# Scan inverse in two 64x64 diagonal parts, in a hybrid encoder layer

## Chip, cores, metric

The kernel runs on one core of one Trainium2 chip. The metric is the device time of one execution in microseconds (us); smaller is better.

## The reference, cut to what matters

One layer: an input projection of x (256 tokens x 1024), three mixers in parallel (gMLP, bidirectional RWKV-7, bidirectional mLSTM), an output projection and a norm, then a mixture of 32 experts and a second norm. The change is in RWKV-7, whose state for each of six heads of 64 channels follows

```python
def _wkv7_step(state, inp):
    r, w, k, v, a, b = inp
    sa = jnp.einsum('phvk,phk->phv', state, a)
    state = state * w[:, :, None, :] + sa[..., None] * b[:, :, None, :] + v[..., None] * k[:, :, None, :]
    return state, jnp.einsum('phvk,phk->phv', state, r)
```

once forward and once backward over the 256 tokens.

## The kernel before

The scan is done in chunks of 128 tokens. Within a chunk the products of keys and queries give a strictly triangular 128x128 matrix M, and the values U that enter the state are the product of the inverse Y of (identity - M) with W, what the earlier state and the values give. A pass handles one pair of heads (`pt` = 0, 1, 2), and in it four matrices (two heads x two chunks, index `j = 2h + c`) for each of two directions `d`.

Y is built by doubling, over `LEVELS = (1, 2, 4, 8, 16, 32, 64)`. Level n joins neighbouring diagonal blocks of m = LEVELS[n] rows and columns to blocks of 2m. `neighbours` (level 0) brings Y with its nearest entries into a bank of PSUM (four matrices x 128 columns = 512 columns) by transposes. At each further level, for each direction: ScalarE has copied Y out of the bank (`turned_in`), with its "late" columns in the first 256 columns of `ym` and its "early" ones in the other 256. TensorE turns the early half (`turn_early`, two transposes) and multiplies the early columns of M by the late ones of Y (`cross`, two matmuls of 128 columns). ScalarE copies the turned half to `tT`; VectorE masks the product to the diagonal blocks (`masked`, 256 columns, into `gm`). `update` adds tT by gm to the late columns of the bank (two matmuls). POOL lays out M's early columns for each level ahead (`early_columns`, four buffers `m_early`). In the profile, a 32-bit matmul appears as two records (two passes), a transpose as one.

Directions are interleaved in an order written out by hand: level n of direction 0, level n of direction 1, then side work of the mLSTM and gMLP mixers (`m_rows`, `scores`, `bonus_sums`, `gate_cols`, `scans_turned` on TensorE, `args` and `factors` on ScalarE, divisions, norms and weights on VectorE), then the updates of both directions. After the levels, two steps over the chunks follow: W (`L1205`, `L1207`), U (`L1219`: Y by W, two matmuls of 64 columns for each direction), the state (`L1226`, `L1227`), and at the end the scan's output (`L1236`, `L1240`, `L1242`). `L1052` is the mLSTM's `weigh`, between W and U of step 0 and also ahead of the neighbours of the later passes; `L1111` are the key products.

Lines of the levels: `L1120` neighbours, `L1128` cross, `L1135` turn_early, `L1143` update, `L799`/`L801` turned_in, `L817` the copy to tT, `L1748` the mask, `L1467` POOL's copies, `L1763` VectorE's masking of the products into `mp`, after which `s_prev` is raised. `L1030` is m_rows, `L1038` scores, `L786` args.

Later: the output projection (`L1257`), the router, and the experts (`L1373` and `L1405` for the two expert matrices, `L1347` combining, `L1357` bias rows), whose weights of 12 MB an expert SyncE loads in pieces into slots as these come free.

Of the kernel before, what the change touches and what calls it, by code (L numbers as in the profile page):

```python
# [14 lines left out]
P = 128  # L15
# [4 lines left out]
HD = 64  # L20
# [14 lines left out]
NL = len(LEVELS)  # L35
# [9 lines left out]
C_BONE = NKEEP  # L45
C_MASK2 = C_BONE + P
C_GM = C_MASK2 + 2 * 3 * P
C_X1 = C_GM + NL * P
C_HSEL = C_X1 + 2 * P
C_SELM = C_HSEL + 2  # L50
# [3 lines left out]
def constants():  # L54

    c = np.zeros((P, NCONST), np.float32)
    i = np.arange(P)
    row, col = i[:, None], i[None, :]
    c[:, C_ID:C_ID + P] = row == col
    c[:, C_TRI0:C_TRI0 + P] = row < col  # L60
    c[:, C_BONE:C_BONE + P] = row // HD == col // HD
    for d in range(2):
        before = (row < col) if d == 0 else (row > col)
        o = C_MASK2 + 3 * P * d
        c[:, o:o + P] = before
        c[:, o + P:o + 2 * P] = before | (row == col)
        c[:, o + 2 * P:o + 3 * P] = before.T
        c[:, C_X1 + d * P:C_X1 + d * P + P] = (row // 2 == col // 2) & (row % 2 == 1 - d) & (col % 2 == d)
    for n, m in enumerate(LEVELS):
        c[:, C_GM + n * P:C_GM + n * P + P] = (row // HD == col // HD) & (row % HD // m == col % HD // m)  # L70
    c[:, C_HSEL:C_HSEL + 2] = row // HD == np.arange(2)[None, :]
    for h in range(RH):
        c[h, C_SELM + h * P:C_SELM + (h + 1) * P] = 1.0
    c[:, C_ONES:C_ONES + P] = 1.0
    c[:, C_IOTA:C_IOTA + P] = np.arange(P)[None, :] % SLOTS
    return c
# [30 lines left out]
def encoder_kernel(nc, t, out, dbg=None):  # L107
# [6 lines left out]
    with ctx:  # L114
# [125 lines left out]

        nqT = rview(2, 0, 2, 4, 256)
        mp = rview(2, 2048, 2, 2, 4, P)
        m_early = [view(o_xT + 512 * b, 2, 2, P) for b in range(4)]
        ym = rview(3, 0, 2, 4, P)
        oT = rview(3, 3584, NCH, P)
        tT = rview(3, 1024, 2, 2, P)
        gm = rview(3, 2048, 2, 2, P)
        bktok = rview(3, 3072, 2, 2, P)

# [91 lines left out]
            a = a.rearrange("p j (b two m) -> p two (j b) m", two=2, m=LEVELS[n])  # L341
            return a if d else a[:, ::-1]

        def by_late(a, d, n):
            return a.rearrange("p j s -> p (j s)").rearrange("p (two b m) -> p two b m", two=2, m=LEVELS[n])

        def half_cols(a, n):

            return a.rearrange("p a (b m) -> p (a b) m", m=LEVELS[n])

        def y_late(d):
            return ym[:, d, 0:2].rearrange("p a (b s) -> p (a b) s", b=2)

        def y_early(d):
            return ym[:, d, 2:4]

        def key_bank(pt, d, h):

# [53 lines left out]
        s_nqe = sem("key_products_evacuated")  # L412
        s_yid = sem("identity_laid")
        s_xup = sem("inverse_evacuated")
        s_me = sem("early_columns_of_operand_ready")
        s_tt = sem("early_columns_turned")
        s_tev = sem("early_columns_evacuated")
# [230 lines left out]
        def _(act):  # L648
# [145 lines left out]
            def turned_in(pt, n, d):  # L794

                act.wait_ge(s_xn, 2 * NL * pt + 2 * n + d + 1)
                y = pview(1 + 4 * d, 0, 4, P)
                if n < NL - 1:
                    A(by_late(ym[:, d], d, n + 1), split(y, d, n + 1), ACT.Copy).then_inc(s_xup, 1)  # L799
                else:  # L800
                    A(ym[:, d], y, ACT.Copy).then_inc(s_xup, 1)  # L801

            def identities():

# [5 lines left out]
            for pt in range(NP):  # L810
                for n in range(1, NL):
                    if n == 1:
                        for d in range(2):
                            turned_in(pt, 0, d)
                    for d in range(2):
                        act.wait_ge(s_tt, 12 * pt + 2 * n + d - 1)
                        A(tT[:, d], pview(4 * d + 2, 0, 2, P), ACT.Copy).then_inc(s_tev, 1)  # L817
                        if n == 2:
                            A(bktok[:, d], pview(4 * d + 2, 256, 2, P), ACT.Copy).then_inc(s_bkev, 1)
                    if n == 3:  # L820
                        if pt == 0:
# [106 lines left out]
        def _(pe):  # L928
# [158 lines left out]
            for pt in range(NP):  # L1087
# [28 lines left out]
                def neighbours(d):  # L1116

                    pe.wait_ge(s_prev, 4 * pt + 2 * d + 2)
                    for j in range(4):
                        last = mm(pview(4 * d + 1, 0, 4, P)[:, j], ym[:, d, j], ident, is_transpose=True, start=(j == 0),  # L1120
                                  stop=False, skip_group_check=True)
                    last.then_inc(s_xn, 1)

                def cross(n, d):

                    pe.wait_ge(s_me, 12 * pt + 2 * n + d - 1)
                    for jj in range(2):
                        last = mm(pview(4 * d, 0, 2, P)[:, jj], m_early[(n - 1) % 4][:, d, jj],  # L1128
                                  y_late(d)[:, 2 * jj:2 * jj + 2], start=True, stop=True)
                    last.then_inc(s_a, 1)  # L1130

                def turn_early(n, d):

                    for jj in range(2):
                        last = tr(pview(4 * d + 2, 0, 2, P)[:, jj], y_early(d)[:, jj], ident)  # L1135
                    last.then_inc(s_tt, 1)

                def update(n, d):

                    pe.wait_ge(s_g, 12 * pt + 2 * n + d - 1)  # L1140
                    pe.wait_ge(s_tev, 12 * pt + 2 * n + d - 1)
                    for jj in range(2):
                        last = mm(part(pview(4 * d + 1, 2 * P * jj, 2, P), n, 1 - d), tT[:, d, jj], gm[:, d, jj],  # L1143
                                  start=False, stop=(n == NL - 1), skip_group_check=True)
                    last.then_inc(s_xn, 1)

                key_products(0)
# [7 lines left out]
                for n in range(1, NL):  # L1155
                    for d in range(2):
                        if n == 1 and d == 1:
                            neighbours(1)
                        if n == 1:
                            pe.wait_ge(s_nqe, 4 * pt + (2 if pt else 1) + d)  # L1160
                        if n == 2:
                            tr(pview(4 * d + 2, 0, 4, P)[:, 2], bt[:, d, d], ident)
                            tr(pview(4 * d + 2, 0, 4, P)[:, 3], kt[:, d, d], ident).then_inc(s_bk, 1)
                        if n == 3:
                            pe.wait_ge(s_bkev, 2 * pt + d + 1)
                        pe.wait_ge(s_xup, 2 * NL * pt + 2 * (n - 1) + d + 1)
                        turn_early(n, d)
                        cross(n, d)
                    if n == 1 and pt == NP - 1:
                        pe.wait_ge(s_gv, 1)  # L1170
                        pe.wait_ge(s_nqe, 4 * pt + 4)
# [26 lines left out]
                for step in range(2):  # L1198
# [13 lines left out]
                    for d in range(2):  # L1212
                        c = d if step == 0 else 1 - d
                        pe.wait_ge(s_wev, 4 * pt + 2 * step + d + 1)
                        if step == 0:
                            pe.wait_ge(s_xup, 2 * NL * pt + 2 * (NL - 1) + d + 1)
                        for h in range(2):
                            j = 2 * h + c
                            last = mm(pview(4 * d + 2, 256, 4, HD)[:, j], ym[:, d, j], wbuf[:, d, j], start=True, stop=True)  # L1219
                        last.then_inc(s_u, 1)  # L1220
                    if step == 0:
                        for d in range(2):
# [212 lines left out]
        def _(pool):  # L1435
# [21 lines left out]

            def early_columns(pt, n):

                if n > 4:  # L1460
                    pool.wait_ge(s_a, 12 * pt + 2 * (n - 4))
                elif n == 1 and pt:
                    pool.wait_ge(s_a, 12 * pt)
                for d in range(2):
                    if n == 1:
                        pool.wait_ge(s_prev, 4 * pt + 2 * d + 2)
                    nc.gpsimd.tensor_copy(half_cols(m_early[(n - 1) % 4][:, d], n), part(mp[:, d, 1], n, d)).then_inc(s_me, 1)  # L1467

            for pt in range(NP):
                if pt == NP - 1:  # L1470
# [1 line left out]
                    pool.dma_start(rw, t["router_w"][0].rearrange("(k p) e -> p k e", p=P)).then_inc(s_rw, 16)  # L1472
                    pool.dma_start(rb, row_bc(t["router_b"][0])).then_inc(s_rw, 16)
                    pool.dma_start(lncol, t["ln1_cols"].rearrange("p (a k) -> p a k", a=2)).then_inc(s_rw, 16)
                for n in range(1, NL):
                    early_columns(pt, n)
                mask_factors(2 * pt)
                mask_factors(2 * pt + 1)
# [14 lines left out]
        def _(dve):  # L1493
# [250 lines left out]
            for pt in range(NP):  # L1744
# [11 lines left out]
                for d in range(2):  # L1756
                    near = scan_const(C_X1 + P * d, P).bitcast(i32)
                    dve.wait_ge(s_yid, 2 * pt + d + 1)
                    for h in range(2):
                        dve.wait_ge(s_prod, 4 * pt + 2 * d + h + 1)  # L1760
                        V.copy_predicated(ym[:, d, 2 * h:2 * h + 2], wide(near, 2), pview(4 * d + h, 0, 2, 2, P)[:, :, 1])
                    for h in range(2):
                        V.tensor_tensor(mp[:, d, :, 2 * h:2 * h + 2].rearrange("p a c s -> p c a s"), pview(4 * d + h, 0, 2, 2, P),  # L1763
                                        wide(mask_mp(d).rearrange("p (a s) -> p a s", a=2), 2), ALU.mult).then_inc(s_prev, 1)
                    if d == 0 and pt:
# [296 lines left out]
```

## Time and profile before

| | |
|---|---|
| median of 3 runs | 1202.96 us (1202.22 to 1203.02) |
| profiled execution: time, span | 1202.76 us, 1200.7 us |
| TensorE busy | 1146.5 us (95% of the span) |
| VectorE, ScalarE, POOL busy | 287.5, 216.5, 32.7 us |
| read from HBM | 429.29 MB, 358 GB/s over the span |
| scan passes end at | 151.9, 190.8, 230.7 us |

Times within the profile count from the start of the span; the profiled execution's time is 2.06 us more than its span. The passes' ends are where the chain of waits leaves the last L1242 of each pass. A busy share is an average over stages, so what a stage is worth has to be read in it.

### The profile page before, as it was taken

The page shows a single profiled execution, that of the slowest core. Times are in us where ns is not written, and L with a number is a line of the kernel's source. Part 1 is how long each engine was busy: PE and PEld are TensorE (multiplying, and loading weights), DVE is VectorE, ACT ScalarE, POOL GpSimd, SP SyncE. Part 2 cuts the span into 40 slices and gives each one's busy share as a digit, 9 for nine tenths or more (in the row PEclk, how much of TensorE's full clock was granted, in tenths as well). Part 3 has the DMA queues.
Part 4 walks back from the last instruction along what each step waited for, and adds up shares of the span by engine and source line. Part 5 has one row for each costly group of instructions (what it writes and reads, how often), then busy time and mean ns, then how long its engine had stood idle before and what let it go on. Part 6 is the DMA issues. An engine that isn't in the chain of part 4 may idle for free.

```text
span 1200.7 us, 14572 instructions
## 1 busy us (share of the span) xinstructions
PE 1146.5 (95%) x5836; PEld 503.0 (42%) x5836; DVE 287.5 (24%) x742; ACT 216.5 (18%) x453; POOL 32.7 (3%) x67
## 2 busy tenths in 40 slices
PE   7999999999999999999999999999999999999995
PEld 6875878753333333333333333333333333333332
DVE  1368566662111111111111111111111111111113
ACT  1345554411111111111111111111111111111112
POOL 1000122100000000000000000000000000000001
PEclk9999999999999999999999999999999999999999
DMA  8525202289999999999999999999999999999994
GB/s 334 201 104 203 101 1 77 111 325 364 408 428 430 428 428 428 428 431 428 428 429 428 428 384 425 429 428 428 428 428 428 428 428 428 428 428 428 427 428 172
DMA packets 34025, 430.69 MB, mean 359 GB/s; under 512 B 3808, under 2 KB 3968, under 8 KB 7888
## 3 DMA queue, kind: packets, MB, share of 16 engines
q1 hardware_dynamic: 32736, 427.15, 84.8%
q0 software_dynamic: 544, 2.06, 0.5%
q10 hardware_dynamic: 720, 1.15, 0.3%
q8 instruction: 16, 0.26, 0.1%
q14 instruction: 9, 0.07, 0.0%
HBM read 429.29 MB, written 1.05 MB: 358 GB/s over the span
## 4 chain that ended last, share of the span: by engine, by line
PE 59%; DMA 32%; DVE 5%; ACT 1%; issue 1%; SPq 1%; POOL 0%; POOLq 0%; DVEq 0%
PE bank L1373 19%; DMA pool<-in_exp_w 17%; DMA ring<-in_exp_w 15%; PE bank L1405 14%; PE bank L958 5%; PE bank L968 3%; PE bank L1347 2%; PE bank L1257 2%; PE bank L1357 2%; PE bank L1391 1%; DVE pool L1974 1%; DVE pool L1969 1%; PE bank L1128 1%; PE bank L1143 1%; DVE pool L1971 1%
## 5 line engine op out<-in xcount | busy, mean ns | idle before, releaser
L1405 PE MATMUL bank<-ring,pool 128*64 128x512 f32 x1024 | 228.4, 596 | 9.3 <-DMA ring<-in_exp_w 9.2
L1373 PE MATMUL bank<-pool 128*64 128x512 f32 x1024 | 228.2, 595 | 7.0 <-DMA pool<-in_exp_w 6.7
L1373 PE MATMUL bank<-ring,pool 128*64 128x512 f32 x1024 | 228.0, 595 | 5.9 <-DMA ring<-in_exp_w 5.6
L1405 PEld LDWEIGHTS bank<-ring,pool 128*64 128x64 f32 x1024 | 70.1, 137 | 165.8 <-issue 145.0
L1373 PEld LDWEIGHTS bank<-pool 128*64 128x64 f32 x1024 | 71.2, 137 | 159.3 <-issue 143.5
L1373 PEld LDWEIGHTS bank<-ring,pool 128*64 128x64 f32 x1024 | 71.2, 137 | 158.1 <-issue 143.1
L1955 DVE TENSOR_SCALAR pool<-pool 128x128 f32<-128x128 f32 x64 | 19.3, 346 | 428.6 <-PE bank L1373 428.6
L898 ACT ACTIVATE pool<-pool 128x512 f32<-128x512 f32 x32 | 20.2, 632 | 473.1 <-DVE pool L1967 473.1
L1967 DVE TENSOR_SCALAR pool<-bank 128x512 f32<-128x512 f32 x32 | 22.2, 693 | 317.6 <-PE bank L1373 317.6
L958 PE MATMUL bank<-pool,ring 128*128 128x256 f32 x272 | 61.4, 388 | 7.1 <-DMA ring<-in_w_in_C 7.1
L1347 PE MATMUL bank<-pool 64*128 64x512 f32 x264 | 65.6, 614 | 0.7 <-ACT pool L908 0.7
L908 ACT ACTIVATE pool<-bank 128x512 f32<-128x512 f32 x32 | 19.2, 599 | 258.3 <-PE bank L1405 258.3
L1333 PE MATMUL bank<-pool 128*64 128x512 f32 x264 | 62.3, 592 | 1.0 <-DVE pool L1928 1.0
L958 PEld LDWEIGHTS bank<-pool,ring 128*128 128x128 f32 x272 | 52.8, 195 | 14.9 <-DMA ring<-in_w_in_C 7.1
L1357 PE MATMUL bank<-pool 32*64 32x512 f32 x392 | 44.8, 613 | 0.0
L1347 PEld LDWEIGHTS bank<-pool 64*128 64x128 f32 x264 | 22.7, 185 | 43.1 <-issue 41.5
L968 PE MATMUL bank<-ring,pool 128*128 128x384 f32 (+2 forms) x96 | 35.3, 528 | 0.0
L1333 PEld LDWEIGHTS bank<-pool 128*64 128x64 f32 x264 | 18.9, 137 | 38.2 <-issue 37.1
L900 ACT ACTIVATE pool<-bank 128x512 f32<-128x512 f32 x32 | 19.2, 599 | 66.4 <-PE bank L1333 66.4
L1969 DVE TENSOR_SCALAR pool<-bank 128x512 f32<-128x512 f32 x32 | 22.2, 693 | 32.8 <-PE bank L1373 32.8
L1257 PE MATMUL bank<-ring,pool 128*128 128x512 f32 x64 | 28.5, 596 | 0.8 <-ACT pool L857 0.8
L1391 PE MATMUL bank<-pool 128*128 128x128 f32 x128 | 24.0, 310 | 3.5
(300 smaller groups left out, 858.2 us busy)
## 6 DMA issues: line engine op xcount, KB each, us to landing
ring<-in_exp_w SPq DMA_DIRECT2D x127, 2048.0 KB, 22.2
pool<-in_exp_w SPq DMA_DIRECT2D x64, 2048.0 KB, 27.0
ring<-in_w_out SPq DMA_DIRECT2D x2, 2048.0 KB, 7.6
ring<-in_w_in_A SPq DMA_DIRECT2D x1, 2048.0 KB, 13.5
ring<-in_w_in_B SPq DMA_DIRECT2D x1, 2048.0 KB, 7.8
ring<-in_w_in_D SPq DMA_DIRECT2D x1, 2048.0 KB, 13.3
ring<-in_w_in_H SPq DMA_DIRECT2D x1, 2048.0 KB, 8.0
ring<-in_exp_w SPq DMA_DIRECT2D x2, 1024.0 KB, 22.3
```

The costliest lines, as they stand in the source:

```text
L898: A(sg, hr, ACT.Sigmoid, scale=1.702).then_inc(s_hs, 1)
L958: last = mm(bank[i % 4][:, 0:S], w[:, k], xT[:, k], start=(k == 0), stop=(k == KD - 1))
L968: last = mm(bank[(NT + j) % 4][:, 0:n], xT[:, k, P * c:P * c + P], w[:, k, :], start=(k == 0), stop=(k == KD - 1))
L1257: last = mm(bank[4 + 2 * c + hf][:, :], xT[:, k, P * c:P * c + P], wout[hf][:, OUT_ORDER[k // 2][k % 2]], start=(k == 0), stop=(k == KD - 1))
L1333: last = mm(bank[7][SLOTS * hf:SLOTS * hf + SLOTS, :], sel[:, c], x_tok[:, c, 512 * hf:512 * hf + 512], start=(c == 0), stop=(c == NCH - 1))
L1347: last = mm(bank[2 * c + hf][:, :], gT[hp, P * c:P * c + P], ysb[hp, :], start=False, stop=stop, skip_group_check=True)
L1357: last = mm(bank[4 + g][SLOTS * hf:SLOTS * hf + SLOTS, :], esel[gp], bias[gp, 512 * hf:512 * hf + 512], start=True, stop=False)
L1373: last = mm(bank[4 + g][hp, :], lhs, w[:, k % 2, o:o + 512], start=False, stop=(k == KD - 1))
L1391: last = tr(pview(4, 0, 4, P)[:, j], hr[:, j:j + 509:4], ident)
L1405: last = mm(bank[6][SLOTS * hf:SLOTS * hf + SLOTS, :], hT[:, k % 4, SLOTS * (k // 4):SLOTS * (k // 4) + SLOTS], w2s[k // 4][:, k % 4, 512 ...
L1967: V.tensor_scalar(hr, bank[4][:, :], 7.0, None, ALU.min).then_inc(s_hg, 1)
L1969: V.tensor_scalar(ur, bank[5][:, :], 7.0, -7.0, ALU.min, ALU.max).then_inc(s_hu, 1)
```

## The change

The inverse is no longer kept as 128x128 until the last level. For the levels up to m = 16 (n = 1 to 5) only its two diagonal 64x64 parts are kept, stacked on the partitions: four matrices x 64 columns = 256 columns of the bank for each direction. The neighbours are now real matmuls with a folding matrix `C_FOLD` (128x64). Each level has one transpose (four matrices x 32 early columns = 128 columns), two products, one for each 64-row block (operand `m_early[:, d, b]`), a mask of 256 columns as before, and two updates of 64 stationary columns into the 64 partitions of their block; the copies by ScalarE are 256 and 128 columns wide instead of 512 and 256. The last level (n = 6) fills the block between the two parts: its operand `m_last` is copied by ScalarE from the products, and its result is `y_last`, with the later diagonal part copied beside it. U is computed by two matmuls instead of one for each matrix: the rows that come first from their own 64x64 part, the later rows from `y_last`. There are three buffers of `m_early` instead of four, and POOL makes two copies instead of one for each level and direction, at five levels instead of six.

```diff
-        m_early = [view(o_xT + 512 * b, 2, 2, P) for b in range(4)]
+        m_early = [view(o_xT + 512 * b, 2, 2, P) for b in range(3)]
+        m_last = view(o_xT + 1536, 2, 4 * HD)
...
             def turned_in(pt, n, d):
                 act.wait_ge(s_xn, 2 * NL * pt + 2 * n + d + 1)
-                y = pview(1 + 4 * d, 0, 4, P)
-                if n < NL - 1:
-                    A(by_late(ym[:, d], d, n + 1), split(y, d, n + 1), ACT.Copy).then_inc(s_xup, 1)
+                if n < NL - 2:
+                    A(by_late(y_blocks(d), n + 1), split(y_bank(d), d, n + 1), ACT.Copy).then_inc(s_xup, 1)
+                elif n == NL - 2:
+                    A(y_blocks(d), bank[4 * d + 1][:, 0:4 * HD], ACT.Copy).then_inc(s_xup, 1)
                 else:
-                    A(ym[:, d], y, ACT.Copy).then_inc(s_xup, 1)
+                    first = rows_of(d)
+                    A(y_last(d)[first], pview(4 * d + 1, 4 * HD, 4, HD)[first], ACT.Copy).then_inc(s_xup, 1)
...
                     if n == 1:
                         for d in range(2):
+                            later, first = rows_of(1 - d), rows_of(d)
+                            for h in (1, 0):
+                                act.wait_ge(s_prev, 4 * pt + 2 * d + 2 - h)
+                                A(m_last[later, d].rearrange("p (j s) -> p j s", j=4)[:, 2 * h:2 * h + 2],
+                                  pview(4 * d + h, 0, 2, 2, P)[later, :, 1, first], ACT.Copy).then_inc(s_ml, 1)
                             turned_in(pt, 0, d)
                     for d in range(2):
                         act.wait_ge(s_tt, 12 * pt + 2 * n + d - 1)
-                        A(tT[:, d], pview(4 * d + 2, 0, 2, P), ACT.Copy).then_inc(s_tev, 1)
+                        A(tT[:, d], bank[4 * d + 2][:, 0:P], ACT.Copy).then_inc(s_tev, 1)
...
+                    if n == NL - 1:
+                        for d in range(2):
+                            later = rows_of(1 - d)
+                            A(y_last(d)[later], y_bank(d)[later], ACT.Copy).then_inc(s_yl, 1)
...
                 def neighbours(d):
                     pe.wait_ge(s_prev, 4 * pt + 2 * d + 2)
+                    pe.wait_ge(s_ml, 4 * pt + 2 * d + 1)
                     for j in range(4):
-                        last = mm(pview(4 * d + 1, 0, 4, P)[:, j], ym[:, d, j], ident, is_transpose=True, start=(j == 0),
-                                  stop=False, skip_group_check=True)
+                        last = mm(y_bank(d)[:, j], ym[:, d, j], scan_const(C_FOLD, HD), start=(j == 0), stop=False,
+                                  skip_group_check=True)
...
+                def level(n, d):
+                    pe.wait_ge(s_me, 10 * pt + 2 * n + d - 1)
+                    if n == 1:
+                        pe.wait_ge(s_ml, 4 * pt + 2 * d + 2)
+                    tr(bank[4 * d + 2][:, 0:P], y_early(d), ident).then_inc(s_tt, 1)
+                    for b in range(2):
+                        last = mm(pview(4 * d, 0, 2, P)[:, b], m_early[(n - 1) % 3][:, d, b], y_late(d), start=True, stop=True)
+                    last.then_inc(s_a, 1)
+
+                def last_level(d):
+                    first, later = rows_of(d), rows_of(1 - d)
                     for jj in range(2):
+                        last = tr(bank[4 * d + 2][:, HD * jj:HD * jj + HD], y_blocks(d)[first, P * jj:P * jj + P],
+                                  ident[first, first])
+                    last.then_inc(s_tt, 1)
+                    for jj in range(2):
+                        last = mm(pview(4 * d, 0, 2, P)[:, jj], m_last[later, d, P * jj:P * jj + P],
+                                  y_blocks(d)[later, P * jj:P * jj + P], start=True, stop=True)
                     last.then_inc(s_a, 1)
...
+                    if n < NL - 1:
+                        for b in range(2):
+                            bp = rows_of(b)
+                            last = mm(part(y_bank(d)[bp], n, 1 - d), tT[:, d, bp], gm[:, d, b], start=False, stop=False,
+                                      skip_group_check=True)
+                    else:
+                        for jj in range(2):
+                            o = 4 * HD + P * jj
+                            last = mm(bank[4 * d + 1][rows_of(d), o:o + P], tT[:, d, HD * jj:HD * jj + HD], gm[:, d, jj],
+                                      start=False, stop=True, skip_group_check=True)
...
                         for h in range(2):
                             j = 2 * h + c
-                            last = mm(pview(4 * d + 2, 256, 4, HD)[:, j], ym[:, d, j], wbuf[:, d, j], start=True, stop=True)
+                            u = pview(4 * d + 2, 256, 4, HD)[:, j]
+                            mm(u[first], y_block(d, j)[first], wbuf[first, d, j], start=True, stop=True)
+                            last = mm(u[later], y_last(d)[:, j], wbuf[:, d, j], start=True, stop=True)
...
                 for d in range(2):
                     if n == 1:
                         pool.wait_ge(s_prev, 4 * pt + 2 * d + 2)
-                    nc.gpsimd.tensor_copy(half_cols(m_early[(n - 1) % 4][:, d], n), part(mp[:, d, 1], n, d)).then_inc(s_me, 1)
+                    m = m_early[(n - 1) % 3][:, d]
+                    for b in range(2):
+                        cols = mp[:, d, 1, :, rows_of(b)].rearrange("p j (b two m) -> p two j b m", two=2, m=LEVELS[n])[:, d]
+                        last = nc.gpsimd.tensor_copy(m[:, b].rearrange("p (j b m) -> p j b m", j=4, m=LEVELS[n]), cols)
+                    last.then_inc(s_me, 1)
```

## Rows read from the trace of the kernel before

**Rows 1.** The page's slices of the span: mean busy share of the DMA engines, in tenths.
```profile
DMA  8525202289999999999999999999999999999994
```

**Rows 2.** Windows of the expert stage: busy time and instructions, clock, DMA share, GB/s.
```profile
400.00:800.00 400.00, 389.15 (x1894) 135.05 (x1891) 53.24 (x127) 44.67 (x84) 0.00 (x0) 1.00 1.00 425
```

**Rows 3.** Timeline of SyncE's DMA queue: start, us, engine, line, operation.
```profile
244.18 0.91 SPq L557 DMA_DIRECT2D pool<-in_exp_w  x2
```

**Rows 4.** Chain of waits, middle pass, its start and levels 1 to 3: start, us, what.
```profile
154.78 1.48 PE bank L1052 x12
156.26 0.45 PE bank L1120 x4
156.70 1.06 PE bank L1111 x8
...
160.69 0.42 DVE ring L1748
...
163.59 0.43 DVE ring L1748
...
164.07 1.16 PE bank L1143 x8
165.23 1.06 PE bank L1030 x4
...
167.63 1.35 ACT pool L786 x4
```

**Rows 5.** Timeline of the middle pass, level 5, direction 0, to level 6.
```profile
173.46 0.44 PE L1135 MATMUL bank<-pool,ring 128*128 128x128 f32 x2 [0.24 <-ACT ring L799]
...
174.45 0.42 DVE L1748 TENSOR_TENSOR ring<-bank,pool 128x256 f32<-128x256 f32 x1 [1.18 <-PE bank L1128]
174.59 0.38 ACT L817 ACTIVATE ring<-bank 128x256 f32<-128x256 f32 x1 [0.28 <-PE bank L1135]
...
175.67 1.20 ACT L799 ACTIVATE ring<-bank 128x512 f32<-128x512 f32 x2 [0.36 <-PE bank L1143]
...
176.32 0.44 PE L1135 MATMUL bank<-pool,ring 128*128 128x128 f32 x2
```

**Rows 6.** Chain of waits, middle pass, from W of step 0 to the scan's output.
```profile
180.02 0.84 PE bank L1207 x8
180.86 1.34 PE bank L1052 x12
182.20 0.89 PE bank L1219 x8
...
186.46 1.04 PE bank L1219 x8
...
188.94 0.42 PE bank L1242 x2
189.36 0.37 PE bank L1236 x4
189.73 0.22 PE bank L1240 x4
```

**Rows 7.** Chain of waits in the expert stage.
```profile
305.90 3.43 PE bank L1373 x16
309.33 1.92 PE bank L1347 x8
```

**Rows 8.** Chain of waits, first pass: VectorE ahead of the second direction's neighbours.
```profile
116.60 1.19 DVE ring L1763 x2
```

**Rows 9.** Groups of instructions of the scan, shapes kept apart: xcount, busy us, mean ns, idle before.
```profile
L1467 POOL COPY pool<-ring 128x256 f32<-128x256 f32 x36 | 13.5, 418 | 119.7 <-DVE ring L1763 112.5 <-PE bank L1128 7.0
L849 ACT ACTIVATE pool<-bank,pool 64x64 f32<-64x64 f32 x12 | 3.7, 308 | 0.5
```

**Rows 10.** Windows of the first pass (columns as in rows 2; clock third from the end).
```profile
127.00:128.00 1.00, 1.00 (x7) 1.00 (x6) 0.16 (x1) 0.38 (x1) 0.00 (x0) 0.50 0.12 49
...
130.00:131.00 1.00, 1.00 (x7) 0.86 (x7) 0.93 (x3) 0.85 (x3) 0.00 (x0) 0.80 0.00 0
```

More of the change, by code:

```diff
@@ L47 @@
 C_GM = C_MASK2 + 2 * 3 * P
+C_FOLD = C_GM
 C_X1 = C_GM + NL * P
@@ L66, in constants @@
         c[:, o + P:o + 2 * P] = before | (row == col)
-        c[:, o + 2 * P:o + 3 * P] = before.T
+        c[:, o + 2 * P:o + 3 * P] = before.T & (row // HD == col // HD)
         c[:, C_X1 + d * P:C_X1 + d * P + P] = (row // 2 == col // 2) & (row % 2 == 1 - d) & (col % 2 == d)
+    c[:, C_FOLD:C_FOLD + HD] = row[:, 0:1] % HD == np.arange(HD)[None, :]
     for n, m in enumerate(LEVELS):
-        c[:, C_GM + n * P:C_GM + n * P + P] = (row // HD == col // HD) & (row % HD // m == col % HD // m)
+        if n:
+            w = HD if n == NL - 1 else HD // 2
+            c[:, C_GM + n * P:C_GM + n * P + P] = (row // w == col // w) & (row % w // m == col % w // m)
     c[:, C_HSEL:C_HSEL + 2] = row // HD == np.arange(2)[None, :]
@@ L242, in encoder_kernel @@
         mp = rview(2, 2048, 2, 2, 4, P)
-        m_early = [view(o_xT + 512 * b, 2, 2, P) for b in range(4)]
+        m_early = [view(o_xT + 512 * b, 2, 2, P) for b in range(3)]
+        m_last = view(o_xT + 1536, 2, 4 * HD)
         ym = rview(3, 0, 2, 4, P)
         oT = rview(3, 3584, NCH, P)
-        tT = rview(3, 1024, 2, 2, P)
+        tT = rview(3, 1024, 2, P)
         gm = rview(3, 2048, 2, 2, P)
@@ L342, in split, with by_late, rows_of, y_blocks @@
             return a if d else a[:, ::-1]
[L344 to L349, printed above, removed]
+        def by_late(a, n):
+            return a.rearrange("p (two b m) -> p two b m", two=2, m=LEVELS[n])
+        def rows_of(b):
+            return slice(HD * b, HD * b + HD)
+        def y_blocks(d):
+            return ym[:, d, 0:2].rearrange("p a (b s) -> p (a b s)", b=2)
+        def y_last(d):
+            return ym[:, d, 2:4].rearrange("p a (b s) -> p (a b) s", b=2)
         def y_late(d):
-            return ym[:, d, 0:2].rearrange("p a (b s) -> p (a b) s", b=2)
+            return y_blocks(d)[:, 0:P]
         def y_early(d):
-            return ym[:, d, 2:4]
+            return y_blocks(d)[:, P:2 * P]
+        def y_block(d, j):
+            return y_blocks(d)[:, HD * j:HD * j + HD]
+        def y_bank(d):
+            return pview(4 * d + 1, 0, 4, HD)
         def key_bank(pt, d, h):
@@ L414, in encoder_kernel @@
         s_xup = sem("inverse_evacuated")
+        s_yl = sem("later_blocks_copied")
+        s_ml = sem("operand_between_blocks_copied")
         s_me = sem("early_columns_of_operand_ready")
@@ L1118, in neighbours @@
                     pe.wait_ge(s_prev, 4 * pt + 2 * d + 2)
+                    pe.wait_ge(s_ml, 4 * pt + 2 * d + 1)
                     for j in range(4):
-                        last = mm(pview(4 * d + 1, 0, 4, P)[:, j], ym[:, d, j], ident, is_transpose=True, start=(j == 0),
-                                  stop=False, skip_group_check=True)
+                        last = mm(y_bank(d)[:, j], ym[:, d, j], scan_const(C_FOLD, HD), start=(j == 0), stop=False,
+                                  skip_group_check=True)
                     last.then_inc(s_xn, 1)
-                def cross(n, d):
-                    pe.wait_ge(s_me, 12 * pt + 2 * n + d - 1)
-                    for jj in range(2):
-                        last = mm(pview(4 * d, 0, 2, P)[:, jj], m_early[(n - 1) % 4][:, d, jj],
-                                  y_late(d)[:, 2 * jj:2 * jj + 2], start=True, stop=True)
+                def level(n, d):
[8 more added lines that the diff above has]
+                    first, later = rows_of(d), rows_of(1 - d)
+                    for jj in range(2):
+                        last = tr(bank[4 * d + 2][:, HD * jj:HD * jj + HD], y_blocks(d)[first, P * jj:P * jj + P],
[4 more added lines that the diff above has]
+                                  y_blocks(d)[later, P * jj:P * jj + P], start=True, stop=True)
                     last.then_inc(s_a, 1)
[L1132 to L1136, printed above, removed]
                 def update(n, d):
@@ L1141, in update @@
                     pe.wait_ge(s_tev, 12 * pt + 2 * n + d - 1)
-                    for jj in range(2):
-                        last = mm(part(pview(4 * d + 1, 2 * P * jj, 2, P), n, 1 - d), tT[:, d, jj], gm[:, d, jj],
-                                  start=False, stop=(n == NL - 1), skip_group_check=True)
+                    if n < NL - 1:
[8 more added lines that the diff above has]
+                                      start=False, stop=True, skip_group_check=True)
                     last.then_inc(s_xn, 1)
@@ L1166, in _ @@
                         pe.wait_ge(s_xup, 2 * NL * pt + 2 * (n - 1) + d + 1)
-                        turn_early(n, d)
-                        cross(n, d)
+                        if n < NL - 1:
+                            level(n, d)
+                        else:
+                            last_level(d)
                     if n == 1 and pt == NP - 1:
@@ L1216, in _ @@
                             pe.wait_ge(s_xup, 2 * NL * pt + 2 * (NL - 1) + d + 1)
+                            pe.wait_ge(s_yl, 2 * pt + d + 1)
+                        first, later = rows_of(d), rows_of(1 - d)
                         for h in range(2):
                             j = 2 * h + c
-                            last = mm(pview(4 * d + 2, 256, 4, HD)[:, j], ym[:, d, j], wbuf[:, d, j], start=True, stop=True)
+                            u = pview(4 * d + 2, 256, 4, HD)[:, j]
+                            mm(u[first], y_block(d, j)[first], wbuf[first, d, j], start=True, stop=True)
+                            last = mm(u[later], y_last(d)[:, j], wbuf[:, d, j], start=True, stop=True)
                         last.then_inc(s_u, 1)
@@ L1458, in early_columns @@
             def early_columns(pt, n):
-                if n > 4:
-                    pool.wait_ge(s_a, 12 * pt + 2 * (n - 4))
+                if n > 3:
+                    pool.wait_ge(s_a, 12 * pt + 2 * (n - 3))
                 elif n == 1 and pt:
@@ L1474, in _ @@
                     pool.dma_start(lncol, t["ln1_cols"].rearrange("p (a k) -> p a k", a=2)).then_inc(s_rw, 16)
-                for n in range(1, NL):
+                for n in range(1, NL - 1):
                     early_columns(pt, n)
@@ L1761, in _ @@
                         V.copy_predicated(ym[:, d, 2 * h:2 * h + 2], wide(near, 2), pview(4 * d + h, 0, 2, 2, P)[:, :, 1])
-                    for h in range(2):
+                    for h in (1, 0):
                         V.tensor_tensor(mp[:, d, :, 2 * h:2 * h + 2].rearrange("p a c s -> p c a s"), pview(4 * d + h, 0, 2, 2, P),
```

## The prediction

> **What bounds the kernel now.** I began with the page's slices. From about a quarter of the span on, the DMA engines are busy in nine tenths or more of every slice [rows 1], and the windows view gives a busy share of 1.00 and 425 GB/s between 400 and 800 us [rows 2]. The expert stage is therefore bound by the stream of its weights. The scan is not in that stage, so the next question is what starts the stream. The DMA queue's timeline answers it: apart from a few early pieces, the expert weights are issued from 244.18 us on [rows 3], behind waits for the last norms and projections. These follow the end of the scan, which is TensorE's program order up to the last `L1242`. The bytes behind that point are fixed, so I count a microsecond of the scan as a microsecond of the kernel, in either direction. The third view is the chain of waits through the scan of one pair of heads. The scan runs three times, once for each pair; its three passes end at 151.9, 190.8 and 230.7 us, and I read the middle one.
>
> Three things in it decide the cost of this change.
>
> At the start and the end of a pass TensorE is never idle for long, and the chain is TensorE's own queue [rows 4, 6]. There each added matmul is paid in full. In the six levels the chain goes round TensorE, VectorE (the mask) and ScalarE (the copies) [rows 5], and side work placed in the levels takes the lead at some of them: VectorE's work between 160.69 and 163.59 us, ScalarE's four `args` (1.35 us), and TensorE's `m_rows` (1.06 us) [rows 4].
>
> The third thing is the time between matmuls of different stationary shapes. A matmul of one pass over 128 columns with 128 stationary columns takes 0.11 us (`L1120`, four in 0.45 [rows 4]), and pairs in different column halves run side by side: `L1240`, four records of 128*64, took 0.22 us. But `L1236` after `L1242` (128*128) took 0.37 us for the same four, and `L1242` took 0.42 us for two records worth 0.22 [rows 6]. `L1052` took 1.48 us behind the 64*128 `L1111` [rows 4] and 1.34 behind the 128*128 `L1207` [rows 6]; `L1347` (64*128) took 1.92 us for eight records between 128*64 ones that need 3.43/16 = 0.214 each, an excess of 0.2 [rows 7]. So every change of shape costs 0.14 to 0.21 us wherever TensorE's queue is full. I take 0.18.
>
> **The change part by part**, for a middle pass.
>
> *Neighbours.* Four transposes (0.45 us [rows 4]) become four real matmuls of 64 columns, thus eight records with 128*128 stationary. The nearest row is `L1219`, eight such records in 0.89 us [rows 6]; with `L1207` at 0.84 I take 0.86, so +0.41 a direction. Bounds: nothing (if the shorter operand makes up for the second pass) and +0.6 (by the 1.04 of the other `L1219`). Both directions lie on TensorE's queue before the first mask that matters: +0.82. Against it stand one transposition instead of two in each direction (0.11 each) and ScalarE's copy of 256 columns instead of 512 (0.38 for 0.60 [rows 5]), 0.22. Sum of the start: +0.38. In the first pass VectorE sets the start of the second direction [rows 8], and only one direction counts: 0.41 - 0.22 - 0.11 = +0.08.
>
> *ScalarE's new copies.* Four `m_last` copies (64x128) and two of `y_last` (64x256) a pass; 0.3 to 0.38 us each by `L849` and the 256-column copy [rows 5, 9]. The first lie in ScalarE's wait for the products, beside VectorE's `L1763`, the last under `m_rows` and the updates of level 6. I cost them at nothing; without that cover the `y_last` pair would cost up to 0.76 us a pass.
>
> *POOL.* Twelve copies a pass of 0.418 us become twenty of half the size [rows 9], between 0.21 and 0.42 each. POOL is idle for 119.7 us ahead of its 36 copies, nearly all of it waiting for a pass to begin, and it runs levels ahead of TensorE; the buffer of level 4 is free once level 1's product is done. Nothing; if a copy of half the size cost the whole 0.42 and came late, 0.4 a pass.
>
> *Level 1 to 2.* From the mask of one to that of the next stands VectorE's division and mean, 160.69 to 163.59 us [rows 4]. No gain.
>
> *Level 2.* The update is 128*64 on both column halves, four records in 0.22 instead of 0.45 [rows 6]. The second direction's mask ends late, so of `L1143`'s 1.16 us about 0.33 goes. In the first pass the masks are early: -0.45, and +0.18 for a shape change behind the 128*128 side work, -0.27.
>
> *Level 3.* ScalarE's order is the chain: both transpositions shorter by 0.11, the copy of `tT` by 0.10, the copy back by 0.22. -0.54.
>
> *Level 4.* TensorE's scores fill the middle. 0.22 of transpositions, 0.23 of the update, 0.22 of the copy back: -0.67. The shape changes stay two in number.
>
> *Level 5.* From 173.46 to 176.32 us there is no side work in front [rows 5]. The mask (174.45, 0.42) and TensorE's queue end together, so only 0.11 comes off before the update; then 0.23 and 0.22, less some 0.1 for the change from 128*128 to 128*64. -0.45.
>
> *Level 6.* Transposes and products keep their count, and overlap by a little because they use different row halves (-0.2); the update leaves TensorE in 128*64 ahead of `L1207` (+0.18). Nothing.
>
> Levels and start together: first pass 0.08 - 0.27 - 0.54 - 0.67 - 0.45 = -1.85; the others 0.38 - 0.33 - 0.54 - 0.67 - 0.45 = -1.61 each. Sum **-5.1 us**.
>
> *U.* This is the part that speaks against the change. Before, each direction and step has two matmuls, four records of 128*128: 0.89 us for both directions in step 0, 1.04 in step 1 [rows 6]. After, each of the two becomes a 64*64 matmul into one half and a 128*64 one into the other, in the order small, large, small, large. The matmul time itself does not grow (sixteen records with half the stationary columns). But the shape changes at every pair of records, eight times a step. A pair of 64 columns in two passes takes 0.107 us; with 0.18 it is 0.29, and eight are 2.3 us. Step 0: +1.41; step 1: +1.26. All of it is on TensorE's queue, since ScalarE's copy of U and everything behind it wait for the last. That is +2.67 a pass, **+8.0 us**. In short it is 16 changes and 1.71 us of matmuls for 1.93. Bounds: at 0.14 a change 16 x 0.14 - 0.22 = 2.02 a pass, 6.1 in all; at 0.21 3.14, 9.4 in all; and zero, because no row shows a change of shape between two matmuls that use different column halves. Each one shown had cells in common with its predecessor. I take the cost as real, because 0.14 to 0.21 is seen for every kind of change the trace has, whether rows or columns changed.
>
> The Trainium skill (TensorEngine Tiling, Key Properties) says that changing the tiling mode, not just the tile, drains TensorE, while tiles of one mode run independently. The rows above agree where they can; whether 64*64 beside 128*64 counts as two modes no row shows. By that rule the sum is the one taken here; were they independent tiles it would be -5.1.
>
> **Sum.** -5.1 + 8.0 = +2.9 us on the profiled execution's 1202.76 us; the median of the runs is 1202.96, so **1205.9 us**.
>
> **Rivals.**
> *The halves of U overlap* (not slower). If matmuls in disjoint column halves don't wait for each other, U costs what it did and the kernel gains 5.1: 1197.9 us. For it: the pairs of `L1240` overlap fully, and none of the shown changes was disjoint. Against it: the changes cost the same for all forms. It decides from a change cost under 0.12 us, where three times 16 x 0.12 - 0.22 is 5.1.
> *The clock falls more often.* In the first pass the granted clock is 0.50 (1.2 GHz) between 127 and about 130.4 us [rows 10], behind a stretch of waits and of small matmuls; at half speed it can cost 1.7 of its 3.4 us, and I take 1.4, since TensorE also waits in it. The levels now hold less matmul work and U has pauses. One more such stretch gives 1207.3, two 1208.7. Against it: the two other passes have a wait of like length and keep 2.4 GHz. The skill (TensorE: Matmul & The Clock Gate, Part 4) says that transposes don't count as busy for the clock; by that the new neighbours, real matmuls, speak against this rival, and no run here shows it.
> *A change is cheaper when the matmuls are short*, half of 0.18: three times 16 x 0.09 - 0.22 is +3.7 instead of +8.0, thus 1201.6 us.
>
> **How the numbers follow.** A difference under 0.2%, 2.4 us, can't be told from none here. Forecast 0.55, own range 1204.0 to 1207.3 (from the bounds of the change cost): 0.33 of it slower, 0.22 the same. Overlap 0.25, all faster. Clock 0.12: 0.10 slower, 0.02 same. Half price 0.08: 0.06 same, 0.02 faster. That gives faster 0.27, same 0.30, slower 0.43. The range, 1197.3 to 1208.4, holds overlap down to a gain of 5.7 and one further clock stretch; what's outside is some 0.13.
>
> **What the profile after would show.** The two groups of U matmuls (64*64 and 128*64) should take about 2.3 us a step in the chain where `L1219` took 0.89 and 1.04; under 1.0 means overlap. Neighbours should be eight records in about 0.86 us. Level 5 should last 2.4 us from transpose to transpose instead of 2.86, its updates four records in 0.22. The masks of levels 1 and 2 stay 2.9 us apart. The end of each pass, and the 244.18 us of the weights' issue, should move by the sum. The prediction is wrong if U's pairs run without pause, if the clock's half-speed stretch moves or multiplies, or if the passes' shift does not reach the end of the stream.

## The result, and the profile after

The changed kernel took 1219.21 us, the median of four runs from 1208.90 to 1226.03; the kernel before took 1202.99 (1202.22 to 1205.43). The ratio is 1.013, with a 95% interval of 1.0102 to 1.0157. It is slower, far outside the range given, and its runs differ by 17 us where those of the kernel before differ by 3. Each run lists its mean granted clock, and the order is that of the times: 0.988 for 1208.90 us, 0.979 for 1217.93, 0.977 for 1220.49, 0.972 for 1226.03. The kernel before has 0.995 to 0.998 in all 46 runs of it that stand beside the experiments below.

The page's slices of the profiled execution (1220.49 us, span 1218.7): clock in tenths of full speed, and DMA.

```profile
PEclk9999787899999999999999999999999999999998
DMA  8425202078999999999999999999999999999994
```

The DMA engines are full from a slice later on [rows 1]; the fifth to the eighth slice, the scan, have the lost clock. The queue's timeline shows where the stream of weights begins:

```profile
262.51 0.99 SPq L579 DMA_DIRECT2D pool<-in_exp_w  x2
```

18.3 us later than in [rows 3], and the span is 18.0 us longer. So the scan's delay reached the end one for one. Windows of the scan (us, PE, PEld, DVE, ACT and POOL busy, clock, DMA share, GB/s):

```profile
136.00:139.00 3.00, 3.00 (x27) 2.28 (x25) 2.62 (x8) 1.73 (x7) 0.00 (x0) 1.00 0.01 3
140.00:159.00 19.00, 18.63 (x107) 14.99 (x108) 3.12 (x12) 3.58 (x11) 1.40 (x2) 0.50 0.00 1
160.00:186.00 26.00, 23.96 (x214) 19.11 (x213) 19.64 (x54) 14.28 (x46) 6.68 (x22) 1.00 0.00 1
188.00:204.00 16.00, 15.63 (x89) 11.99 (x90) 4.46 (x15) 2.90 (x10) 3.06 (x5) 0.50 0.05 10
222.00:231.00 9.00, 8.88 (x43) 7.00 (x42) 4.35 (x12) 4.82 (x15) 1.45 (x2) 0.50 0.00 0
```

TensorE ran at 1.2 GHz in the second, fourth and fifth of these windows. With their edges the three stretches last 20.5, 17.1 and 10.2 us, 47.8 us in all, where the kernel before had one of 3.4 in its scan [rows 10]. The clock fell at 139.4 and 187.2 us, right behind level 6 with its `m_rows` and W and before any matmul of U in that pass, and at 221.4 us in level 3, behind a wait of 0.93 us for VectorE and an `m_rows`. It came back in the scan's output, at 159.9 and 204.3 us, and in level 5 at 231.6 us. TensorE counts as busy for 98% of the half-speed windows and for all of the three microseconds from 136 to 139, right ahead of the first fall. Idle time doesn't explain the first two falls.

The middle pass up to its U ran mostly at full clock and can be read against [rows 4 to 6]. The chain of waits, here `L1131` the first work of the pass, `L1807` the mask, `L1163` and `L1172` the transposes, `L1192` the last update, `L1258` W, `L1085` weigh, `L1273` and `L1274` the two halves of U:

```profile
160.11 1.99 PE bank L1131 x32
...
169.25 0.42 DVE ring L1807
...
172.16 0.44 DVE ring L1807
...
174.46 0.26 PE bank L1163
...
177.16 0.33 PE bank L1163
...
180.40 0.33 PE bank L1163
...
182.69 0.27 PE bank L1172
...
184.95 0.59 PE bank L1192 x8
185.54 1.03 PE bank L1258 x8
186.57 1.86 PE bank L1085 x12
188.43 0.40 PE bank L1273 x2
188.84 0.40 PE bank L1274 x2
...
238.24 0.26 PE bank L1273 x2
238.50 0.26 PE bank L1274 x2
```

From the end of the previous pass to the end of the last update this pass took 25.4 us (160.1 to 185.5), where the one before took 28.1 (151.9 to 180.0): -2.7. Each pair of U took 0.26 us at full clock, in the third pass, and 0.40 at half. So both terms of the prediction's sum are there, and a third, much larger one is on top.

### The profile page after: what moved, and what is told of

It is laid out like the page before. It is cut to its first block, busy times and chain, and to the rows that moved or that the text cites. A ratio compares the mean times of both kernels' runs of the same rounds, so it can differ in the third digit from the quotient of the medians.

```text
span 1218.7 us, 14728 instructions
## 1 busy us (share of the span) xinstructions
PE 1164.1 (96%) x5878; PEld 510.7 (42%) x5878; DVE 287.6 (24%) x742; ACT 210.3 (17%) x471; POOL 35.2 (3%) x91
## 3 DMA queue, kind: packets, MB, share of 16 engines
q0 software_dynamic: 544, 2.06, 0.5%
## 4 chain that ended last, share of the span: by engine, by line
PE 62%; DMA 30%; DVE 5%; issue 1%; ACT 1%; SPq 1%; POOL 0%; POOLq 0%; DVEq 0%
PE bank L1428 20%; DMA pool<-in_exp_w 17%; PE bank L1460 14%; DMA ring<-in_exp_w 13%; PE bank L991 5%; PE bank L1001 3%; PE bank L1402 3%; PE bank L1412 2%; PE bank L1312 2%; PE bank L1446 1%; DVE pool L2033 1%; DVE pool L2028 1%; DVE pool L2030 1%; PE bank L1165 1%; PE bank L1396 1%
```

## The experiments

**U split alone.** The kernel before with U's two-shape matmuls:

```diff
+                        first, later = slice(HD * d, HD * d + HD), slice(HD * (1 - d), HD * (1 - d) + HD)
...
-                            last = mm(pview(4 * d + 2, 256, 4, HD)[:, j], ym[:, d, j], wbuf[:, d, j], start=True, stop=True)
+                            u = pview(4 * d + 2, 256, 4, HD)[:, j]
+                            mm(u[first], ym[first, d, j, first], wbuf[first, d, j], start=True, stop=True)
+                            last = mm(u[later], ym[:, d, j, later], wbuf[:, d, j], start=True, stop=True)
```

> The kernel before with only U changed: each matrix's 128*128 matmul becomes a 64*64 one and a 128*64 one, in the order of the changed kernel. Shape changes alone: the changed kernel's pairs at full clock take 0.26 us, 8 a step are 2.06 us against 0.89 and 1.04, so +2.2 a pass, +6.6 in all, 1209.6 us, mean clock as before (0.996). Theory P (the pauses in U pull the clock down and keep it down): clock 0.98 to 0.99 and 1213 to 1220 us. Theory L (the thinner levels start the falls, U only prolongs them): clock at least 0.993, 1209 to 1211 us.

Measured: 1209.71 us (five runs, 1208.91 to 1209.90) against 1202.85, ratio 1.0054 (1.0041 to 1.0067), clock 0.996 to 0.998. Its chain in the middle pass, then its clock in a window of the scan:

```profile
183.92 0.26 PE bank L1221 x2
184.17 0.26 PE bank L1222 x2
184.43 0.25 PE bank L1221 x2
```

```profile
120.00:160.00 40.00, 38.34 (x329) 32.16 (x328) 22.93 (x57) 19.70 (x50) 5.90 (x12) 1.00 0.19 80
```

Eight pairs of 0.26 us a step are there and the kernel is 6.9 us slower; the clock did not fall. With the levels of the kernel before, the pauses are a price of their own and start no fall. Theory P falls for these levels. The one half-speed stretch of [rows 10] isn't in this profile, so it is not in every execution of these levels.

**The levels with U in one shape.** The changed kernel, with W's first rows copied once more, over zeros in the others, so that the first half of U is 128*64 too:

```diff
+            A(wfirst.rearrange("p d h e -> p (d h) e"), ident[:, 0:HD].unsqueeze(1).broadcast_to([P, 4, HD]), ACT.Copy, scale=0.0)
...
+                        A(wfirst[rows_of(d), d], pview(4 * d, 0, 2, HD)[rows_of(d)], ACT.Copy)
                         A(wbuf[:, d, c::2], pview(4 * d, 0, 2, HD), ACT.Copy).then_inc(s_wev, 1)
...
-                            mm(u[first], y_block(d, j)[first], wbuf[first, d, j], start=True, stop=True)
+                            mm(u[first], y_block(d, j), wfirst[:, d, h], start=True, stop=True)
```

> The changed kernel, but U's first half is also a 128*64 matmul: its right operand is a copy of W whose later rows are zero, made by one more ScalarE copy of 64 partitions for each direction and step (about 0.3 us, partly on the path). No shape changes inside U; the halves should pair up, 0.22 us for four records of 64 columns or less. The levels gave 2.5 us a pass at full clock (160.1 to 186.6 us against 151.9 to 180.9 before). Theory P: clock 0.994 or more, 1203.0 - 7.5 + 1 = 1196.5 us. Theory L: the falls at the levels' end remain but heal sooner, clock 0.985 to 0.992, 1199 to 1207 us.

Measured: 1206.69 us, the median of twelve runs from 1200.22 to 1218.15, clock 0.975 to 0.989; ratio 1.003 (1.0004 to 1.0056). The falls come without any shape change in U. The slices of the clock in its profiled execution (1201.50 us, clock 0.988, one of the milder runs), and the window of the lost clock:

```profile
PEclk9999999799999999999999999999999999999998
```

```profile
213.00:229.00 16.00, 15.60 (x112) 13.10 (x111) 4.94 (x17) 4.74 (x16) 1.40 (x2) 0.50 0.00 1
```

The clock fell at 212.4 us, again behind level 6 of a pass, with its W and ahead of its U; the stretch of [rows 10] is there too, at 127.5 us. Theory L is right that the changed levels start the falls; which of their parts does is not separated. Whether U's pauses prolong them stays open: the changed kernel's 0.972 to 0.988 and these runs' clocks overlap.

**m_rows on 128 rows**, in the changed kernel and in the kernel before. The selecting operand is zero beyond its 6 rows, so the results stay. Here is the edit of both:

```diff
-                    last = mm(bank[3][:, S * d:S * d + S], scan_const(C_SELM + P * h, P)[0:RH],
-                              row1[0:RH, d], start=True, stop=True)
+                    last = mm(bank[3][:, S * d:S * d + S], scan_const(C_SELM + P * h, P),
+                              row1[:, d], start=True, stop=True)
```

> The changed kernel, with m_rows (six calls, four records of 6*128 each) on all 128 rows: the selecting operand is zero in the other 122 rows, so the result is the same. Two shape changes a call go where the neighbours are 128*128, one where an update follows. Price alone: 6 x 0.18 to 6 x 0.36, 1 to 2 us less. If the clock counts how much of the array is used, those 1.05 us stretches now count in full: Theory R (rows count) expects the falls at the end of the levels to go, clock 0.99 or more, 1200 to 1208 us. If only busy time counts, clock unchanged at 0.97 to 0.98, about 1217 us.

In the changed kernel, measured: 1201.79 us, twelve runs from 1199.75 to 1203.96, clock 0.995 to 0.997; ratio to the kernel before 0.9991 (0.9982 to 1.0000). Seventeen microseconds came back from a change that removes no matmul. Its windows, and its chain in the middle pass, from `L1131` of that pass to `L1131` of the next:

```profile
120.00:160.00 40.00, 36.97 (x340) 29.71 (x338) 24.69 (x61) 18.73 (x59) 9.77 (x27) 1.00 0.18 74
160.00:200.00 40.00, 37.67 (x346) 30.67 (x345) 26.63 (x77) 19.29 (x62) 10.43 (x29) 1.00 0.17 58
200.00:230.00 30.00, 27.80 (x235) 22.18 (x234) 17.62 (x55) 14.30 (x47) 4.07 (x8) 0.94 0.01 1
```

```profile
150.23 1.99 PE bank L1131 x32
...
163.51 1.06 PE bank L1063 x4
164.57 0.11 PE bank L1163
...
173.85 1.06 PE bank L1063 x4
...
188.68 1.99 PE bank L1131 x32
```

TensorE is busy for less of these windows than in the half-speed ones above, and keeps 2.4 GHz but for one stretch of 3.4 us in the third pass. The middle pass, at full clock, took 38.45 us, against 38.9 in the kernel before. `m_rows` (`L1063`) still takes 1.06 us in level 6, between products of 64*128 and an update of 128*64; only in level 2 does the edit save a change of shape, since the transpose behind it (`L1163`, 0.11 us for 0.26) is 128*128 too. That is 0.15 us a pass.

> The kernel before with m_rows on all 128 rows. It prices a shape change by itself: before, every call stands between 128*128 matmuls, so two changes of 0.18 us go at each of six calls, 2.2 us: 1200.8 us. If the changes cost nothing and the excess seen in the chain is the matmul's own, 1203.0. By theory R the one half-speed stretch between 127 and 130.4 us also goes, another 1.4 us: 1199.4.

In the kernel before, measured: 1200.11 us, eleven runs from 1199.02 to 1202.40, ratio 0.9977 (0.9968 to 0.9985), clock 0.997 to 0.998. Its chain in level 2 and behind level 6:

```profile
164.41 0.86 PE bank L1030 x4
165.28 0.22 PE bank L1135 x2
...
176.73 0.86 PE bank L1030 x4
177.59 0.89 PE bank L1143 x8
```

The same update in the kernel before:

```profile
178.93 1.09 PE bank L1143 x8
```

`m_rows` went from 1.06 to 0.86 us [rows 4], and the update behind it from 1.09 to 0.89 for eight records. That is 0.2 for each change of shape, as the prediction read it. The whole is -2.7 us, 0.5 more than the 2.2 expected of the changes. The half-speed stretch of [rows 10] is not in its profile either, but one profile can't tell whether the edit removed it.

**m_rows on 64 rows**, in the changed kernel: the same edit with `[0:64]`.

> The changed kernel with m_rows on 64 rows instead of 6. It has exactly the shape changes of the changed kernel (64*128 between 128*128 and 128*64), but ten times the rows in use. Theory R (the clock counts the array's rows in use): most falls gone, clock 0.99 or more, 1200 to 1206 us. Theory S (the two shape changes saved at each call were what kept the clock in the 128-row run): clock 0.97 to 0.985 and 1209 to 1226 us, like the changed kernel.

Measured: 1203.42 us, eleven runs from 1199.61 to 1204.72, clock 0.994 to 0.997. Its windows, and its chain in levels 2 and 6 of the middle pass:

```profile
120.00:160.00 40.00, 37.08 (x339) 29.96 (x339) 24.62 (x60) 18.81 (x60) 10.07 (x28) 1.00 0.20 85
160.00:200.00 40.00, 37.52 (x331) 30.18 (x330) 25.20 (x71) 18.88 (x60) 10.03 (x27) 0.96 0.17 58
200.00:230.00 30.00, 27.80 (x233) 21.90 (x232) 19.60 (x62) 14.87 (x48) 5.08 (x12) 0.96 0.01 1
```

```profile
164.37 1.06 PE bank L1063 x4
165.43 0.26 PE bank L1163
...
174.86 0.86 PE bank L1063 x4
175.73 0.59 PE bank L1192 x8
```

Two stretches of 3.4 us at half speed are left, in the second and the third pass. The expectation has every shape change in place, but in level 6 the products ahead of `m_rows` are 64*128 too, and one change a pass goes (0.86 us for 1.06); those in level 2 stay. The runs on 64 and on 128 rows each save one change of shape a pass, but not the same one: on 128 rows level 6, behind which the clock fell twice, is timed as in the changed kernel (1.06, then 0.59). What both share is the rows that the six calls use. The number of changes doesn't order the clocks either: U split alone has more of them and keeps it, U in one shape has fewer and loses it. So theory S falls, though no run changed the rows with every shape change in place. The runs on 64 rows, and the two below, were taken on another chip than those above. The kernel before is the same on both (1202.85 and 1203.12 us), but the levels with `m_rows` on 6 rows were not run on this second chip.

**U grouped**, with m_rows on 128 rows: the two 64*64 matmuls of a direction first, then the two 128*64 ones.

```diff
                             u = pview(4 * d + 2, 256, 4, HD)[:, j]
                             mm(u[first], y_block(d, j)[first], wbuf[first, d, j], start=True, stop=True)
+                        for h in range(2):
+                            j = 2 * h + c
+                            u = pview(4 * d + 2, 256, 4, HD)[:, j]
                             last = mm(u[later], y_last(d)[:, j], wbuf[:, d, j], start=True, stop=True)
```

> The changed kernel with m_rows on 128 rows, and U's two small matmuls issued together, then the two large ones: four shape changes a step instead of eight, the work unchanged. If the price sits on each change, a step takes 4 x (0.107 + 0.21) = 1.3 us or, with 0.15 a change, 1.5 instead of 2.06: 6 x 0.6 to 0.8, 3.4 to 4.7 us below the 128-row run, 1197 to 1198.5 us. If 64*64 matmuls are slow in themselves, no difference: 1201.8.

Measured: 1197.01 us (six runs, 1196.24 to 1201.05), clock 0.996 to 0.998, ratio 0.9952 (0.9938 to 0.9966), 4.8 us below the run with eight changes a step. Its chain, step 0 of the middle pass:

```profile
177.88 0.37 PE bank L1273 x4
178.25 0.38 PE bank L1277 x4
178.62 0.37 PE bank L1273 x4
179.00 0.39 PE bank L1277 x4
```

Two pairs now take 0.37 us where they took 0.52: half as many changes, 0.15 less for each one saved.

**U in one shape, m_rows on 128 rows.** Once level 6 has read them, ScalarE writes zeros over the later rows of the first blocks, so W needs no further copy:

```diff
-                            A(y_last(d)[later], y_bank(d)[later], ACT.Copy).then_inc(s_yl, 1)
+                            A(y_last(d)[later], y_bank(d)[later], ACT.Copy)
+                            act.wait_ge(s_a, 12 * pt + 11 + d)
+                            A(ym[later, d, 0:2], ident[later].unsqueeze(1).broadcast_to([HD, 2, P]), ACT.Copy, scale=0.0).then_inc(s_yl, 1)
...
-                            mm(u[first], y_block(d, j)[first], wbuf[first, d, j], start=True, stop=True)
+                            mm(u[first], y_block(d, j), wbuf[:, d, j], start=True, stop=True)
```

> The changed kernel with m_rows on 128 rows, and U in one shape at no extra copy of W: once level 6 has read them, ScalarE writes zeros over the later rows of the first blocks, so both matmuls of U are 128*64. In the run with the padded W a step's sixteen records took about 0.5 us against 2.06 split and 0.89 before. From m_rows alone (1201.8): 6 x 1.5 less, some of it taken by the wait for W's copy in step 1: 1193 to 1194 us if the clock holds at 0.995 or more. If it was the pauses' absence or presence and not the rows that moved the clock, the falls of the padded run return: 0.98 to 0.99 and 1195 to 1205.

Measured: 1192.83 us (five runs, 1191.70 to 1193.69) against 1203.12, ratio 0.9912 (0.9899 to 0.9924), clock 0.997 to 0.998. Chain in the middle pass, and groups of U in its scan:

```profile
174.75 1.34 PE bank L1087 x12
176.09 0.20 PE bank L1275
...
176.52 0.29 ACT pool L878
```

```profile
L1275 PE MATMUL bank<-pool,ring 128*64 128x64 f32 x48 | 4.7, 231 | 0.0
L1276 PE MATMUL bank<-pool,ring 128*64 128x64 f32 x48 | 4.7, 231 | 0.0
```

From the end of weigh to ScalarE's copy U takes 0.4 us for both directions, against 2.06 split and 0.89 before. The whole is 9.0 us below the 128-row run, a little more than the 7.8 to 8.8 expected. This version beats the kernel before by 10 us and the changed kernel by 26.

## Why the prediction was wrong

**The step that failed is the rival of the clock.** The prediction said "one more such stretch gives 1207.3, two 1208.7", gave it 0.12, and let the forecast keep the clock of the kernel before. The profile after has 47.8 us at half speed, in three stretches, and its execution is 17.7 us longer than the profiled one of before. The evidence against this rival, that the two other passes keep 2.4 GHz, was read as room; but [rows 10] showed that one pass did lose the clock, and the change takes matmul work out of exactly these levels. The real matmuls of the neighbours, which the prediction counted against this rival, did not keep the clock. I also took a stretch's length to be that of the one seen, 3.4 us, and lowered its cost because TensorE waits in it, where the windows of [rows 10] have it busy throughout. In the changed kernel a stretch lasts up to 20.5 us. An estimate of what is left without it: by the changed kernel's own runs, 17.1 us between clocks 0.988 and 0.972, it would stand near 1200.3 us at the 0.996 of the kernel before. The 128-row run, at 1201.8, agrees within 2 us; 0.45 of it (three times 0.15) is the gain of `m_rows` itself.

**U: mechanism right, term too large.** The forecast was +8.0 us, 0.29 a pair. Measured alone it is +6.9, 0.26 a pair, and the grouped and one-shape runs show that the price sits on the change of shape. The rival of overlapping halves fell: 64*64 and 128*64 in different column halves do wait for each other. The prediction named this as the one case that no row of before showed. The rule of the Trainium skill (TensorEngine Tiling, Key Properties), that changing the mode drains the array while tiles of one mode are independent, agrees with both measurements: 2.06 us split, 0.4 us in one shape. The half-price rival fell too.

**Levels: too small a gain.** The forecast was -1.61 a middle pass; to the start of W it was -2.7. Two starts of the kernel before are needed beside [rows 4 to 6], of levels 3 and 4:

```profile
166.28 0.37 PE bank L1135 x2
...
169.52 0.44 PE bank L1135 x2
```

The start (+0.4), the unmoved 2.9 us between the first masks, level 2 (-0.39 for -0.33), level 3 (177.16 from 174.46, 2.70 instead of 3.24: -0.54) and level 4 (3.24 instead of 3.94: -0.70) came as worked out. Level 5 gave -0.57 for -0.45. Level 6 was put at nothing and gave 0.85: its transposes and products, on different row halves, overlap, and the updates of the two directions, now in different column halves, ran in 0.59 us where `L1143` had 1.09. The change of shape ahead of W cost its 0.19 (1.03 for 0.84 [rows 6]).

**The stream** followed one for one, as forecast. The copies by ScalarE and POOL that were costed at nothing leave no piece of their own in the chain of the levels. Without the clock the sum, an estimate that takes the middle pass for all three (-2.7 and the 0.19 of W), would have been about -7.5 + 6.9, near no change, and not the slight loss that was forecast. The 128-row run bears this out: its middle pass is 0.3 us shorter than that of the kernel before, once the 0.15 of `m_rows` is taken off.

## What to carry to other kernels

Where TensorE's queue is full, count the changes of stationary shape as well as the matmuls: each costs 0.15 to 0.2 us, and padding an operand with zeros to keep one shape paid 9 us here. Before thinning a stage, look for any half-speed stretch in it: here there was one of 3.4 us in these levels, and thinning them by 2.5 us a pass cost some seventeen. Look also for matmuls that use few rows: zeros in the other rows cost no time here. And a kernel whose runs spread by 17 us at different mean clocks should be compared at equal clock, before its structure is blamed.

## What was not expected of the hardware

The clock stayed down for up to 20.5 us with TensorE 98% busy by the profile, in stages that ran at 2.4 GHz in the profile of the kernel before. With the changed levels, six calls of matmuls that use 6 of 128 rows decided it: on 6 rows the mean clock was 0.972 to 0.988, on 64 rows 0.994 to 0.997, on 128 rows 0.995 to 0.997. The 24 records of these calls were busy for 6.8, 6.5 and 6.8 us. Why the rows matter no run shows.

The Trainium skill (TensorE: Matmul & The Clock Gate, Why this matters for your kernels) names idle gaps between bursts of matmuls as what lowers the clock. Here the split of U, which adds pauses of about 0.15 us but no long gap, left it at 0.996 to 0.998. The longest waits of TensorE in the two passes ahead of the first two falls, 0.69 and 0.55 us, are in the 128-row run too (0.69 and 0.54), which kept the clock there. The 0.93 us ahead of the third are in the 64-row run too, where the clock fell only 23 us later, at 227.7 us. So on this case the rule is not enough.

Sixteen records of 128*64 with 64 columns in alternating halves took about 0.4 us, half of what eight records of 128*128 took for the same product.
